# Inverse deviations of the attention and HGRN heads on VectorE, by bit arithmetic and Newton steps, in place of ScalarE's square root

## What is computed

```python
def rms_norm(x, g):
    xf = x.astype(F32)
    y = xf * lax.rsqrt(jnp.mean(xf * xf, axis=-1, keepdims=True) + EPS)
    return (y * g.astype(F32)).astype(x.dtype)
...
    out = rms_norm(out, subln_g) * (1.0 - lam_init)          # attention, per token and head
...
    o = rms_norm(o, norm_g) * jax.nn.sigmoid(g...)           # HGRN, per token and head
```

## Time and profile before

| what | value |
|---|---|
| median of three runs | 2212.87 us |
| the profiled execution: span from first to last instruction | 2209.1 us |
| TensorE busy | 1838.8 us, 83% |
| VectorE busy | 426.9 us, 19%, 973 instructions |
| ScalarE busy | 256.8 us, 12%, 602 instructions |
| the chain that ended last | PE 56%, DMA 37%, DVE 3%, ACT 1% |

### The profile page before, as it was taken

One profiled execution on the slowest core, in us unless ns is written; L12 is line 12 of the kernel. 1 busy time (PEld: TensorE's weight loads), 2 busy tenths in 40 slices (PEclk: granted clock), 3 DMA queues, 4 the chain that ended last, 5 costly groups with the idle time before them and its releaser, 6 DMA issues.

```text
span 2209.1 us, 30075 instructions
## 1 busy us (share of the span) xinstructions
PE 1838.8 (83%) x13111; PEld 1073.7 (49%) x13111; DVE 426.9 (19%) x973; ACT 256.8 (12%) x602; POOL 161.8 (7%) x206
## 2 busy tenths in 40 slices
PE   7959999999999999999829777777877787787871
PEld 6425489966668568999713222222222222222220
DVE  3211332326425222000251000000000000000005
ACT  2001111110134223101200000000000000000002
POOL 2313323000000000000010000000000000000000
PEclk9979999999999999999959998998999989899995
DMA  6432333231122142222249999999999999999986
GB/s 175 101 83 76 92 78 92 57 99 51 45 58 72 50 146 56 65 72 77 96 205 422 425 422 422 413 424 412 405 416 397 422 400 424 414 416 423 413 338 252
DMA packets 185726, 525.00 MB, mean 238 GB/s; under 512 B 20374, under 2 KB 144458, under 8 KB 147440
## 3 DMA queue, kind: packets, MB, share of 16 engines
q1 hardware_dynamic: 164640, 493.44, 57.3%
q0 software_dynamic: 8976, 24.49, 3.6%
q10 hardware_dynamic: 11968, 4.89, 1.0%
HBM read 510.42 MB, written 29.75 MB: 245 GB/s over the span
## 4 chain that ended last, share of the span: by engine, by line
PE 56%; DMA 37%; DVE 3%; ACT 1%; another core or an unknown queue 1%; issue 1%; SPq 1%; POOLq 0%; DVEq 0%; POOL 0%; ACTq 0%
PE psum L673 20%; PE psum L687 18%; DMA arena<-in_moe_w_gate 12%; DMA arena<-in_moe_w_down 11%; DMA arena<-in_moe_w_up 11%; PE psum L900 7%; PE psum L917 3%; PE psum L779 2%; PE psum L712 1%; DVE arena L1181 1%; PE psum L810 1%; PE psum L838 1%; DMA arena<-expert_rows 1%; PE psum L823 1%
## 5 line engine op out<-in xcount | busy, mean ns | idle before, releaser
L900 PE MATMUL psum<-arena 128*32 128x512 f32 x4096 | 509.5, 648 | 171.9 <-DMA arena<-in_moe_w_gate 63.1
L673 PE MATMUL psum<-arena 128*128 128x128 f32 x3968 | 452.5, 276 | 0.0
L673 PEld LDWEIGHTS psum<-arena 128*128 128x128 f32 x3968 | 449.0, 193 | 2.2 <-issue 1.7
L687 PE MATMUL psum<-arena 128*128 128x512 f32 x914 | 404.2, 599 | 26.6 <-DMA arena<-in_w_in 23.0
L900 PEld LDWEIGHTS psum<-arena 128*32 128x32 f32 x4096 | 160.3, 118 | 520.6 <-issue 520.6
L687 PEld LDWEIGHTS psum<-arena 128*128 128x128 f32 x914 | 172.6, 192 | 233.1 <-issue 232.7
L917 PE MATMUL psum<-arena 128*32 128x512 f32 x2048 | 229.8, 601 | 48.4 <-DMA arena<-in_moe_w_down 48.2
L917 PEld LDWEIGHTS psum<-arena 128*32 128x32 f32 x2048 | 71.8, 111 | 194.8 <-issue 194.7
L1181 DVE TENSOR_TENSOR arena<-arena 128x128 f32<-128x128 f32 (+15 forms) x395 | 141.7, 404 | 22.5 <-ACT arena L971 14.3
L1181 DVE TENSOR_TENSOR arena<-arena,psum 128x512 f32<-128x512 f32 (+2 forms) x21 | 12.0, 574 | 672.0 <-PE psum L900 671.9
L971 ACT ACTIVATE arena<-psum 128x512 f32<-128x512 f32 (+4 forms) x118 | 60.6, 536 | 510.5 <-PE psum L687 262.1
(11 more groups left out here) (187 smaller groups left out, 891.3 us busy)
## 6 DMA issues: line engine op xcount, KB each, us to landing
arena<-in_moe_w_gate SPq DMA_DIRECT2D x64, 2048.0 KB, 28.9
arena<-in_moe_w_up SPq DMA_DIRECT2D x64, 2048.0 KB, 33.5
arena<-in_moe_w_down SPq DMA_DIRECT2D x64, 2048.0 KB, 28.3
arena<-in_w_in SPq DMA_DIRECT2D x43, 1024.0 KB, 6.1
arena<-in_w_out SPq DMA_DIRECT2D x16, 1024.0 KB, 7.0
arena<-in_x SPq DMA_DIRECT2D x8, 1024.0 KB, 10.5
arena<-expert_rows SPq DMA_DIRECT2D x8, 1024.0 KB, 13.6
hs_rows<-arena SPq DMA_DIRECT2D x4, 1024.0 KB, 4.6
```

The costliest lines, as they stand in the source:

```text
L673: last = mm(B(bank, [(1, P)], off=quarter * P), F(lhs + k * S + quarter * P, P), F(slot + k * P, P), start=(k == 0), stop=(k == KD - 1))
L687: last = mm(B(bank, [(1, S)]), F(slot + k * P, P), F(rhs + k * S, S), start=(k == 0), stop=(k == n - 1))
L900: last = mm(B(bank, [(1, FE)], 32 * g, 32), F(XT + c * CAP + 32 * g, 32), F(SLOT[slot] + (c % 8) * FE, FE), start=(c == 0), stop=(c == KD ...
```

## The change

For the attention and HGRN heads `deviation` is split. ScalarE keeps the four squares (`squares`) and signals at the last of them. The Sqrt goes, and VectorE's reciprocal goes too. A new function on VectorE, `rsqrt`, takes the sums: mean plus EPS, a shift of the bits by one, the magic constant less the shifted bits (integers), and four Newton steps of three instructions. These are 15 dependent instructions over 128x4 elements, each settled. The row norms at the start, ahead of the experts and at the end keep ScalarE's Sqrt.

```diff
+        RTA = take(TB)
...
+            def squares(srcs, junk, ss, scales=None):
...
+                    last = A(junk, x, ACT.Square, accum_out=F(ss + i, 1), **kw)
+                    if i + 1 < len(srcs):
+                        last.then_inc(act_step, 1)
+                        n_step[0] += 1
+                        act.wait_ge(act_step, n_step[0])
+                return last
...
-                    deviation([B(bank, [(1, P)], off=t * P) for t in range(TB)], F(HSQ, P), SM + 16, HST,
-                              HD).then_inc(ho_std, 1)
+                    squares([B(bank, [(1, P)], off=t * P) for t in range(TB)], F(HSQ, P), SM + 16).then_inc(ho_std, 1)
...
-                    deviation([B(7, [(1, P)], off=t * P) for t in range(TB)], F(ASQ, P), SM + 20, HST + TB, AV,
-                              R0 + (h % 2) * TB).then_inc(ao_std, 1)
+                    squares([B(7, [(1, P)], off=t * P) for t in range(TB)], F(ASQ, P), SM + 20,
+                            R0 + (h % 2) * TB).then_inc(ao_std, 1)
...
+            def rsqrt(x, root, half, width):
+
+                settle(ts(F(x, TB), F(x, TB), 1.0 / width, EPS, M, AD))
+                settle(ts(F(root, TB).bitcast(I32), F(x, TB).bitcast(I32), 1, None, ALU.logical_shift_right))
+                settle(ts(F(root, TB).bitcast(I32), F(root, TB).bitcast(I32), -1.0, 1597463007.0, M, AD))
+                for _ in range(4):
+                    settle(tt(F(half, TB), F(root, TB), F(root, TB), M))
+                    settle(v.scalar_tensor_tensor(F(half, TB), F(half, TB), -0.5, F(x, TB), M, M))
+                    settle(v.scalar_tensor_tensor(F(root, TB), F(half, TB), 1.5, F(root, TB), AD, M))
...
-                settle(v.reciprocal(F(HST, TB), F(HST, TB)))
+                rsqrt(SM + 16, HST, RTA, HD)
...
-                settle(v.reciprocal(F(HST + TB, TB), F(HST + TB, TB)))
+                rsqrt(SM + 20, HST + TB, RTA, AV)
```

More of the change, by code:

```diff
@@ L973, in _, with deviation @@
             n_step = [0]
-            def deviation(srcs, junk, ss, sd, width, scales=None):
+            def squares(srcs, junk, ss, scales=None):
                 for i, x in enumerate(srcs):
                     kw = {} if scales is None else {"scale": F(scales + i, 1)}
-                    A(junk, x, ACT.Square, accum_out=F(ss + i, 1), **kw).then_inc(act_step, 1)
-                    n_step[0] += 1
-                    act.wait_ge(act_step, n_step[0])
+                    last = A(junk, x, ACT.Square, accum_out=F(ss + i, 1), **kw)
[4 more added lines that the diff above has]
+                return last
+            def deviation(srcs, junk, ss, sd, width, scales=None):
+                squares(srcs, junk, ss, scales).then_inc(act_step, 1)
+                n_step[0] += 1
+                act.wait_ge(act_step, n_step[0])
                 return A(F(sd, len(srcs)), F(ss, len(srcs)), ACT.Sqrt, scale=1.0 / width, bias=F(EPSC, 1))
```

## The result

| | median | from, to |
|---|---|---|
| before, 20 runs | 2212.68 us | 2207.3 to 2222.68 |
| changed, 20 runs | 2221.4 us | 2219.03 to 2225.62 |

The ratio is 1.0036 (95% interval 1.0026 to 1.0046): the changed kernel is slower by 8.0 us of 2213, give or take 2.2 (the two medians lie 8.7 apart). The forecast was 2220.7 us in a range of 2216.0 to 2225.0. The kernel before scatters by 15 us over its 20 runs, the changed one by 7; single profiles are therefore read by their waits and not by their ends. The changed kernel's profiled execution has a span of 2220.2 us.

What follows compares the result with a forecast made beforehand. TensorE was taken as the bounding engine in the first half, edits counting where it idles. Waits and row norm, 3.45 + 0.55 + 1.15 + 0 + 1.0 = 6.15 us, plus clock 1.7 gave 7.85: 2220.7 us, range 2216.0 to 2225.0.

Steps and rivals of the forecast that it cites:

- The growth of a head, 1.15 us: Attention head: 15 instructions 0.20 us apart plus hand-over replace 1.96 us of table load and Sqrt, 1.15 us longer.
- the upper bound of 0.30: Upper bound in us for one chain instruction: longest settled distance, 0.20, and half as much again for a conversion.
- Heads one to three, 3.45 us: First three attention heads: TensorE already waits 2.4 us for bank 7, so growth goes straight through, 3 x 1.15 us.
- Heads four and five, 0.55 us: Attention heads four and five: 1.02 us of cover leaves 0.15 at four; later softmax weights make 0.4 at five.
- Head six, 1.15 us: Last attention head: nothing covers the chain, TensorE already waits 1.9 us for the transpose's input; 1.15 us more.
- HGRN at zero: HGRN heads: they back up at 6.2 us a head but stay hidden, 1.6 us of cover left; cost zero.
- Row norm, 1.0 us: Row norm ahead of the experts: its Sqrt must now load the table itself and starts 1.0 us later.
- The clock, 1.7 us, bounds 0 and 6: TensorE after the last head's longer wait: one more clock fall in about half of executions, 1.7 us added once.
- A dearer table switch (1): Rival: some 1.3 us more per ScalarE table switch than recorded cancels the heads' 1.15; time about 2215 us; chance 0.05.
- A quick chain (2): Rival: VectorE's chain instructions take 0.07 us, TensorE's waits shrink; -8.7 us, time 2204 us; chance 0.05.
- dear integers (3): Rival: integer or small instructions in VectorE's chain cost over 0.22 us; at 0.30, +21 us, 2234 us; chance 0.05.
- The clock taking it back (4): Rival: median run has one TensorE clock fall fewer, so 6.15 shows as 3 to 4.4 us, 2216 to 2217.2; chance 0.15.

Runs made afterwards that it cites:

- Eight steps: The changed kernel with eight Newton steps in place of four, 27 instructions in the chain: 2250.47 us, ratio 1.0153 to the kernel before.
- two Newton steps: The changed kernel with two Newton steps in place of four, 9 instructions in the chain: 2212.78 us, ratio 0.9989 to the kernel before.
- two banks on the kernel before: The kernel before, with PSUM banks 7 and 4 in turn for attention outputs and four small banks in place of five: 2211.24 us, ratio 0.9991.

## Why the prediction was right

The time, 2221.4 us, lies 0.7 us from the forecast, and the mechanism is the one forecast: VectorE's chain lengthens TensorE's waits, and the row norm pays for a table load. Part of the closeness is luck, as the point on the clock says.

- *The growth of a head, 1.15 us.* Right: 1.14 at the first head, and the waits at heads two and three went from 2.45 to 3.60. What carried it was the distance of settled instructions (0.20 in the earlier trace rows, 0.197 measured) in place of their duration. The integer instructions, which no row showed, took the same 0.2 us. A slip that changes nothing: the longest settled distance in the rows is 0.21, not the 0.20 from which the upper bound of 0.30 was taken.
- *Heads one to three, 3.45 us.* Measured 1.50 + 1.15 + 1.15. The extra 0.35 us at the first is VectorE's: its TENSOR_REDUCE started 0.46 us late behind its own logits (at 682.63). The profile before has the same once, at another unit (650.44), and three more profiles here have one such wait 0.35 us longer than the rest. What causes it is open.
- *Heads four and five, 0.55 us.* 0.29 and 0.44, together 0.73; 0.15 and 0.4 were forecast. At head five the total was right and its place was not: VectorE's logits start at 848.12, 0.45 us later than the shift ahead of them, as worked out, but TensorE had already lost 0.38 us at the bank, where 0.15 was forecast, and so its wait for the weights stayed at 0.4 us.
- *Head six, 1.15 us.* Measured 1.16.
- *HGRN at zero.* Right, shown by the version with these heads alone, with 6.17 us for a head where I had 6.2 and 1.75 us of cover where I had 1.6. Eight steps showed that it ends there.
- *Row norm, 1.0 us.* Measured 1.02, and given back by loading the table early.
- *The clock, 1.7 us, bounds 0 and 6.* The term was too small. The fall after the last head came in every profile with the long chain, not in half; and it came in two of five profiles in which that wait was 1.9 us (two Newton steps, two banks on the kernel before), so that the one profile read for the prediction, without it, did not show that 1.9 us leaves the clock up. By the profiles' means the term is 4.0 us. With the 6.7 us of waits and row norm that makes some 10.7 us, more than the 8.0 measured (give or take 2.2), and where the difference went is not shown. That the sum of 7.85 fell so near 8.0 is therefore in part luck: the runs of the kernel before scatter by 15 us, profiles with its waits lost between 1.7 and 6.5 us to the low clock, and the times don't resolve 2 us. In the one pair of profiles of the first result the clock differs by 0.8 us only, since the profile before had three falls.
- *Rivals.* A dearer table switch (1) is out: 1.28 us and nothing more, at both places, and with all loads put back the time stood. A quick chain (2) and dear integers (3) are out at 0.197 us. The clock taking it back (4) did not happen; it adds.

## What to carry to other kernels

Price a chain of dependent small instructions by the distance of their starts, 0.2 us here whatever they compute, and hold that against the one thing it replaces: nine of them were a table load and a Sqrt, fifteen were 1.15 us more. Ask of an engine that is relieved whether anything waits for it, and of a removed table load who inherits it: here the row norm did. A stall on TensorE costs itself and then, where the clock falls, the matmuls behind it at half rate: lengthening the waits from 2.4 to 3.6 us cost about 4 us over four places beyond the waits by the means of the profiles, and filling the holes gave 8.6 us back (give or take 3.9).

## What was not expected

- Filling TensorE's idle time with matmuls of no use is worth 0.39% here (give or take 0.18), as much as the whole change costs.
- Under the wait for bank 7 lay two others (1.7 of 2.4 us, and 2.85 of 3.6), for ScalarE's evacuation and for VectorE's logits, which appeared one after the other as each was uncovered.
